# Delta rule's doubling steps: only the nonzero blocks masked, copied and multiplied

## The reference, cut to what matters

```python
kk = jnp.einsum("bhncd,bhnsd->bhncs", k, k)
a_mat = jnp.where(strict, kk * decay * beta[..., :, None], 0.0)
lhs = jnp.eye(CHUNK, dtype=jnp.float32) + a_mat
rhs = jnp.concatenate([v * beta[..., None], k * (beta * jnp.exp(G))[..., None]], axis=-1)
sol = lax.linalg.triangular_solve(lhs, rhs, left_side=True, lower=True, unit_diagonal=True)
```

## Time and profile before

| | |
|---|---|
| time, median of 3 runs | 2549.62 us (2547.74 to 2551.56) |
| profiled execution, its span (first to last instruction; no other time of it is given) | 2549.4 us |
| PE busy | 2211.0 us, 87% |
| DVE busy | 1752.8 us, 69% |
| ACT busy | 1001.0 us, 39% |
| granted TensorE clock, mean | 0.936 of 2.4 GHz |
| records of line 1352 (products of the delta rule) | 944 of 13768 on PE |

### The profile page before, as it was taken

One profiled execution on the slowest core, in us unless ns is written; L12 is line 12 of the kernel. 1 busy time (PEld: TensorE's weight loads), 2 busy tenths in 40 slices (PEclk: granted clock), 3 DMA queues, 4 the chain that ended last, 5 costly groups with the idle time before them and its releaser, 6 DMA issues.

```text
span 2549.4 us, 34445 instructions
## 1 busy us (share of the span) xinstructions
PE 2211.0 (87%) x13768; PEld 1900.7 (75%) x13768; DVE 1752.8 (69%) x3280; ACT 1001.0 (39%) x1607; POOL 806.2 (32%) x673
## 2 busy tenths in 40 slices
PE   8999999999999999999999999999998554444445
PEld 8999998999999999998999998888875221111112
DVE  6656895566556556895566556243559999899986
ACT  4446554554345446563555432443322111111111
POOL 1006871000000006871000000000037777777774
PEclk9999999999999999999999999999999777777767
DMA  7568994035555568993035554443469999999997
GB/s 244 185 173 145 188 181 137 20 119 174 183 183 172 191 163 153 178 185 133 18 118 168 191 187 155 131 143 107 162 217 407 419 419 419 418 420 419 420 419 325
DMA packets 316513, 560.29 MB, mean 220 GB/s; under 512 B 16312, under 2 KB 233410, under 8 KB 316354
## 3 DMA queue, kind: packets, MB, share of 16 engines
q1 hardware_dynamic: 242626, 289.63, 41.2%
q0 software_dynamic: 73728, 268.47, 25.9%
HBM read 557.00 MB, written 1.05 MB: 219 GB/s over the span
## 4 chain that ended last, share of the span: by engine, by line
PE 63%; DVE 17%; POOL 8%; DMA 7%; issue 3%; ACT 2%; SPq 0%; DVEq 0%; ACTq 0%; POOLq 0%
PE banks_to L945 11%; DVE banks_to L1159 7%; PE bank L459 6%; PE bank L460 6%; PE bank L461 6%; PE bank L368 6%; DMA proj<-in_peer_v,gdn_conv 4%; POOL proj L2843 4%; POOL weights L2843 3%; PE banks_and L368 3%; DMA weights<-in_peer_v,gdn_conv 3%; PE banks_to L1352 2%; PE banks_and L459 2%; PE banks_and L460 2%; PE banks_and L461 2%
## 5 line engine op out<-in xcount | busy, mean ns | idle before, releaser
L415 POOL TENSOR_TENSOR weights_low<-weights,weights_high 128x1024 fp32r<-128x1024 f32 x128 | 306.0, 2427 | 649.8 <-ACT weights_high L378 630.4
L461 PE MATMUL bank<-operand_hi,weights_low 128*128 128x256 f32 x1744 | 492.1, 282 | 0.0
L459 PE MATMUL bank<-operand_hi,weights_high 128*128 128x256 f32 x1728 | 488.7, 283 | 0.3 <-DVE gdn_conv L1244 0.2
L460 PE MATMUL bank<-operand_lo,weights_high 128*128 128x256 f32 x1728 | 487.4, 282 | 0.0
L378 ACT CAST weights_high<-weights 128x1024 fp32r<-128x1024 f32 x392 | 386.3, 1045 | 0.8 <-DMA weights<-in_ffn_w_in 0.7
L451 DVE TENSOR_TENSOR weights_low<-weights,weights_high 128x1024 fp32r<-128x1024 f32 x264 | 308.2, 1222 | 93.5 <-ACT weights_high L378 93.5
L461 PEld LDWEIGHTS bank<-operand_hi,weights_low 128*128 128x128 f32 x1744 | 330.5, 190 | 0.0
L459 PEld LDWEIGHTS bank<-operand_hi,weights_high 128*128 128x128 f32 x1728 | 327.1, 189 | 3.0 <-issue 0.8
L460 PEld LDWEIGHTS bank<-operand_lo,weights_high 128*128 128x128 f32 x1728 | 325.7, 188 | 1.2
L461 PE MATMUL banks_and<-operand_hi,weights_low 128*128 128x256 f32 x720 | 202.8, 282 | 0.0
L459 PE MATMUL banks_and<-operand_hi,weights_high 128*128 128x256 f32 x704 | 199.2, 283 | 0.3 <-DVE gdn_conv L1244 0.2
(11 more groups left out here) (574 smaller groups left out, 4675.3 us busy)
## 6 DMA issues: line engine op xcount, KB each, us to landing
weights<-in_ffn_w_in SPq DMA_DIRECT2D x88, 1024.0 KB, 5.1
weights<-in_mix_w_in SPq DMA_DIRECT2D x64, 1024.0 KB, 12.9
weights<-in_ffn_w_out SPq DMA_DIRECT2D x44, 1024.0 KB, 5.0
weights<-in_w_in SPq DMA_DIRECT2D x24, 1024.0 KB, 5.4
weights<-in_cnv_w_o SPq DMA_DIRECT2D x8, 1024.0 KB, 6.2
weights<-in_gdn_w_o SPq DMA_DIRECT2D x8, 1024.0 KB, 5.2
weights<-in_mix_w_out SPq DMA_DIRECT2D x8, 1024.0 KB, 5.0
proj<-in_peer_w_q SPq DMA_DIRECT2D x5, 1024.0 KB, 11.6
```

What stands on the lines that cost most here:

```text
L415: S.rest.by(X.gpsimd.tensor_tensor(halves(m.low[b % SLOTS])[q], halves(m.raw[b % SLOTS])[q], halves(mix_high(m, l, i))[q].bitcast(F32), AL ...
L459: t.matmul(out, w_hi, x_hi, start=start, stop=False, skip_group_check=skip)
L460: t.matmul(out, w_hi, x_lo, start=False, stop=False, skip_group_check=skip)
L461: return t.matmul(out, w_lo, x_hi, start=False, stop=stop, skip_group_check=skip)
```

## The change

Every operation of a doubling step is cut to the columns and rows that are not zero.

- The masked keys of steps 2 to 6 are packed: half the columns (64 of 128) go to the first half of `KB` (`Delta.L`). DVE masks 512 elements per partition instead of 1024.
- The first product streams only the 64 columns of T whose bit k is 0 (all steps), and from step 2 on it loads only the 64 packed columns as weights, so its result is 64 x 64. ACT copies 256 elements per group instead of 512, from step 2 on in 64 partitions.
- The transposes of steps 2 to 5 are made of the other 64 columns of T, which DVE packs with a new copy into the second half of `KB` (`Delta.Tc`); PE waits for that copy ("Tc"). The transpose has 64 partitions; ACT copies 64 partitions x 512. Step 6 transposes all of T as before.
- The second product streams 64 columns; its weights are 128 columns of `TT` as before, in steps 2 to 5 in 64 partitions. In step 6 it is 64 x 64, in partitions 64 to 127.
- DVE subtracts 256 elements per group instead of 512.

The diff, cut:

```diff
+        thin = lambda t: t.rearrange("p j n -> p (j n)").rearrange("p (half j n) -> p half j n", half=2, n=P // 2)
+        self.L, self.Tc = ([thin(B["KB"])[:, half, :, :] for B in m.delta] for half in range(2))
...
+    def bit(t, k, value):
+        return t.rearrange("p j (a two b) -> p (j a) two b", two=2, b=1 << k)[:, :, value, :]
...
+STEP = P // 2
+def step_rows(k):
+    return slice(0, P) if k == 1 else slice(STEP, P) if k == 6 else slice(0, STEP)
...
@@ vector_level
-    mask = m.level[:, k, :].unsqueeze(1).to_broadcast([P, 8, P])
-    S.delta_dve.by(X.vector.tensor_tensor(m.delta[g]["KB"], m.delta[g]["A"], mask, ALU.mult), l, "L", k, g)
+    if k < 2:
...
+    else:
+        four = lambda t: t.rearrange("p j (a b) -> p j a b", b=1 << k)
+        A = Delta.bit(m.delta[g]["A"], k, 1).rearrange("p (j a) b -> p j a b", j=8)
+        mask = Delta.bit(m.level[:, k:k + 1, :], k, 1).unsqueeze(1).to_broadcast([P, 8, STEP >> k, 1 << k])
+        ins = X.vector.tensor_tensor(four(Delta(m).L[g]), A, mask, ALU.mult)
@@ tensor_delta
-            E.by(products(X, m.four(b), lambda j: B["KB"][:, 4 * c + j, :], lambda j: B["T"][:, 4 * c + j, :]), l, "M", k, g, c)
+            out = m.four(b)[:, :, 0:STEP] if k == 1 else m.four(b)[0:STEP, :, 0:STEP]
+            keys, upper = B["KB"] if k == 1 else D.L[g], D.bit(D.ch(B["T"], c), k, 0).rearrange("p (j a) b -> p j a b", j=4)
+            E.by(products(X, out, lambda j: keys[:, 4 * c + j, :], lambda j: upper[:, j, :, :]), l, "M", k, g, c)
...
+                if k < 6:
+                    w.wait_ge(*V.at(l, "Tc", k, g, c))
...
+                        ins = t.transpose(m.four(b + 2)[0:STEP, j, :], D.Tc[g][:, 4 * c + j, :], m.ident[:, :])
...
-                E.by(products(X, m.four(b + 2), lambda j: B["TT"][:, 4 * c + j, :], lambda j: B["D"][:, 4 * c + j, :]), l, "TM", k, g, c)
+                E.by(products(X, m.four(b + 2)[:, :, 0:STEP], lambda j: B["TT"][rows, 4 * c + j, :],
+                              lambda j: B["D"][rows, 4 * c + j, 0:STEP]), l, "TM", k, g, c)
...
+                E.by(products(X, m.four(b + 2)[0:STEP, :, 0:STEP], lambda j: B["D"][rows, 4 * c + j, 0:STEP],
+                              lambda j: B["TT"][rows, 4 * c + j, STEP:P]), l, "MT", g, c)
@@ vector_delta
+                V.by(v.tensor_tensor(upper4, upper4, step, ALU.subtract), l, "T", k, g, c)
+                if k < 5:
+                    w.wait_ge(*V.at(l, "T", k, g, c))
+                    V.by(v.tensor_copy(ch(D.Tc[g], c).rearrange("p j (a b) -> p (j a) b", b=2 << k), Delta.bit(ch(B["T"], c), k + 1, 1)),
+                         l, "Tc", k + 1, g, c)
@@ scalar_delta
-            A.by(a.copy(D.ch(B["D"], c), m.four(b)), l, "M", k, g, c)
+            A.by(a.copy(D.ch(B["D"], c)[step_rows(k), :, 0:STEP], m.four(b)[out, :, 0:STEP]), l, "M", k, g, c)
...
-                A.by(a.copy(D.ch(B["TT"], c), m.four(b + 2)), l, "TT", k - 1, g, c)
+                A.by(a.copy(D.ch(B["TT"], c)[rows, :, :], m.four(b + 2)[rows, :, :]), l, "TT", k - 1, g, c)
```

More of the change, by code:

```diff
@@ L1342, in ch @@
         return t[:, 4 * c:4 * c + 4, :]
+    @staticmethod
+    def bit(t, k, value):
+        return t.rearrange("p j (a two b) -> p (j a) two b", two=2, b=1 << k)[:, :, value, :]
 GC = [(g, c) for g in range(2) for c in range(2)]
@@ L1589, in tensor_delta @@
                 X.bank_free(b + 2)
+                if k < 6:
+                    w.wait_ge(*V.at(l, "Tc", k, g, c))
                 for j in range(4):
-                    ins = t.transpose(m.four(b + 2)[:, j, :], B["T"][:, 4 * c + j, :], m.ident[:, :])
+                    if k < 6:
+                        ins = t.transpose(m.four(b + 2)[0:STEP, j, :], D.Tc[g][:, 4 * c + j, :], m.ident[:, :])
+                    else:
+                        ins = t.transpose(m.four(b + 2)[:, j, :], B["T"][:, 4 * c + j, :], m.ident[:, :])
                 E.by(ins, l, "turned", k - 1, g, c)
@@ L1598, in tensor_delta @@
             X.bank_free(b + 2)
+            rows = step_rows(k)
             if k < 6:
-                E.by(products(X, m.four(b + 2), lambda j: B["TT"][:, 4 * c + j, :], lambda j: B["D"][:, 4 * c + j, :]), l, "TM", k, g, c)
+                E.by(products(X, m.four(b + 2)[:, :, 0:STEP], lambda j: B["TT"][rows, 4 * c + j, :],
+                              lambda j: B["D"][rows, 4 * c + j, 0:STEP]), l, "TM", k, g, c)
                 X.free[b + 2] = [V.at(l, "T", k, g, c)]
             else:
-                E.by(products(X, m.four(b + 2), lambda j: B["D"][:, 4 * c + j, :], lambda j: B["TT"][:, 4 * c + j, :]), l, "MT", g, c)
+                E.by(products(X, m.four(b + 2)[0:STEP, :, 0:STEP], lambda j: B["D"][rows, 4 * c + j, 0:STEP],
+                              lambda j: B["TT"][rows, 4 * c + j, STEP:P]), l, "MT", g, c)
                 X.free[b + 2] = [V.at(l, "TT", 6, g, c)]
@@ L1661, in vector_delta @@
 def vector_delta(X, m, S, l):
-    v, w, conv, L = X.vector, X.dve, m.conv, m.layer[l]
+    v, w, conv, L, D = X.vector, X.dve, m.conv, m.layer[l], Delta(m)
     E, A, V, ch = S.delta_pe, S.delta_act, S.delta_dve, Delta.ch
@@ L1683, in vector_delta @@
                 w.wait_ge(*E.at(l, "TM", k, g, c))
-                V.by(v.tensor_tensor(ch(B["T"], c), ch(B["T"], c), m.four(b + 2), ALU.subtract), l, "T", k, g, c)
+                upper, step = Delta.bit(ch(B["T"], c), k, 0), m.four(b + 2)[:, :, 0:STEP].rearrange("p j (a b) -> p j a b", b=1 << k)
+                upper4 = upper.rearrange("p (j a) b -> p j a b", j=4)
+                V.by(v.tensor_tensor(upper4, upper4, step, ALU.subtract), l, "T", k, g, c)
[3 more added lines that the diff above has]
+                         l, "Tc", k + 1, g, c)
             else:
                 w.wait_ge(*E.at(l, "MT", g, c))
-                V.by(v.tensor_tensor(ch(B["TT"], c), ch(B["TT"], c), m.four(b + 2), ALU.subtract), l, "TT", 6, g, c)
+                corner = ch(B["TT"], c)[0:STEP, :, STEP:P]
+                V.by(v.tensor_tensor(corner, corner, m.four(b + 2)[0:STEP, :, 0:STEP], ALU.subtract), l, "TT", 6, g, c)
     vector_out_rest(X, m, S, l, 0)
@@ L1714, in scalar_delta @@
             w.wait_ge(*V.at(l, "QK", g, c))
-            A.by(a.copy(D.ch(B["D"], c), m.four(b)), l, "M", k, g, c)
+            out = slice(0, P) if k == 1 else slice(0, STEP)
+            A.by(a.copy(D.ch(B["D"], c)[step_rows(k), :, 0:STEP], m.four(b)[out, :, 0:STEP]), l, "M", k, g, c)
             if k > 1:
+                rows = step_rows(k) if k < 6 else slice(0, P)
                 w.wait_ge(*E.at(l, "turned", k - 1, g, c))
-                A.by(a.copy(D.ch(B["TT"], c), m.four(b + 2)), l, "TT", k - 1, g, c)
+                A.by(a.copy(D.ch(B["TT"], c)[rows, :, :], m.four(b + 2)[rows, :, :]), l, "TT", k - 1, g, c)
         if k < 6:
```

3 lines of the change are left out of this document (added).

## The result

| | before | changed |
|---|---|---|
| median | 2550.63 us (5 runs) | 2564.93 us (5 runs, 2555.48 to 2566.57) |
| ratio to before | | 1.0049, 95% interval 1.0039 to 1.006 |
| span of the profiled execution | 2549.4 us | 2557.2 us (its time 2558.63) |
| granted clock, mean of the profiled execution | 0.936 | 0.931 |

The forecast was 2543.0 us, faster, with 2532 to 2558 as the range. The kernel became slower. The five times of the changed kernel lie 11 us apart, those of before 4, and their mean clocks go from 0.931 (2558.63 and 2555.48 us) to 0.924 (2566.57 us): the ratio in the table is the one on record for these runs, and that of the two medians is 1.0056. By either the kernel is slower by about half a per cent, clear of the noise.

The account below looks back on a forecast made before the run. PE was taken to bound the kernel: 10.1 us gained on narrow products less 6.8 us for form changes is 3.3 us per layer, 6.6 for both, giving 2543.0 us from 2549.6; range 2532 to 2558 us.

Parts of the forecast that it names:

- What bounds the kernel: In the steps PE has no idle time; only PE's work, waits or pace move the end.
- The pace of a record: On PE, a record gets cheaper only if loaded and streamed columns both shrink: 0.059 us at 64, against 0.111.
- The gain of 0.42 per group: First products of steps 2 to 6 and step 6's second products: 24 groups, 10.1 us per layer.
- the form change of 0.13: Narrow products alternate with full-form transposes in steps 2 to 6: 10 changes per step, 6.8 us lost per layer.
- the sum: Over the steps, 10.1 less 6.8 gives 3.3 us per layer, 6.6 for both: 2543.0 us.
- DVE and ACT: Masks, subtractions and copies in the steps stay covered by PE; DVE goes from 5.2 to 4.35 us per step.
- the fourth rival: Less dense PE work in the steps lowers the granted clock; eight spells give 2556 us; chance 0.12.
- the fewer rows: Second products on 64 partitions load the same number of columns, so they stay at 0.89 us per group: gain 0.
- the eight spells of the text: Half-clock spells of 3.4 us, each losing 1.6 us in the steps; eight in all give 2556 us.
- Third rival: Each form change in the steps costs a record's whole latency, 0.275 us: slower, 2556.9 us; chance 0.15.
- First and second rival: No form changes with narrow transposes: 2535.8 us, chance 0.17; changes free or second products shrink too: 2532 us, chance 0.08.
- Fifth rival: Gains and gaps in the steps cancel: within 0.2%, the lower edge of the forecast's own case; no separate chance.

Follow-up runs that it names:

- the run with 72 columns: Changed kernel with second products streaming 128 columns; first products of steps 2 to 6 also load 72 columns instead of 64: 2535.49 us, ratio 0.9946.
- the wide kernel: Changed kernel, but second products of steps 1 to 5 stream 128 columns, and step 1's first products all of T: 2543.21 us, ratio 0.9979.
- the one with all rows: Kernel loading 72 columns with ACT's other work moved earlier, plus second products of steps 2 to 5 on 128 rows, unused ones cleared: 2533.17 us, ratio 0.9936.

## Why the prediction was wrong

**What bounds the kernel: right.** PE's pace in the steps decided every run.

**The pace of a record: right.** 0.059 was forecast and 0.058 measured; the second products stayed at 0.89 per group; neither side alone helps. The gain of 0.42 per group and the form change of 0.13 (measured 0.12 to 0.15, and 0.19 at the change of rows) gave 3.3 us per layer; with the clock held up the gain was 66.62 - 63.58 = 3.04, and the time 2543.21, where 2543.0 stood. That is a match of the sum in a kernel with wide second products, not of the forecast for this one. The reading of the earlier trace rows, that transposes run in the full form and that the narrow products change form 10 times a step, is what the run with 72 columns showed.

**DVE and ACT: right.** Covered, with the durations taken.

**The step that failed is the granted clock: the sum takes 1.00 throughout, the fourth rival, given 0.12, was the case that occurred, and the fewer rows were costed at nothing.** The price of a spell was near (1.6 us for 3.4 us at half clock); there was more of it than the eight spells of the text. The clock cost about 7.06 us in layer 0 and 10.16 in layer 1 of the profiled execution (span 2557.2), where the sum had a gain of 6.6 for both; the slower executions were up to 8 us longer, at a lower mean clock. The evidence was misread in three ways. The earlier trace rows show 40 loaded columns at full clock, but those products use 128 rows and stream 256 columns, so they say nothing of products that use half of both. The text weighed "loads and gaps", while the runs show that the size of the second products counts, rows and streamed columns together: the gaps and narrow first products of the wide kernel did no harm, and full first products did not protect. And the fewer rows stand in the words "The fewer rows (64 partitions) change nothing in the number of columns loaded". That holds for the pace, and for the clock it was most of the harm: the same edit with 128 rows is 2544.4 us, with other numbers in the unused rows. Not all of it: the spell in step 1 of layer 1 had no product on 64 rows before it in its stretch.

Three smaller readings were wrong and changed nothing. The 0.275 us for a record's latency is the mean duration of a product record of line 1352, not in the earlier trace rows. Step 5 of layer 0 began at 493.55 us, not 493.3. And the fillers of the earlier trace rows do not start at the fast pace: 24 in 3.17 us is 0.13 each, and the first stand 0.21 apart (9.40, 9.62, 9.83 us), so they do not show that transposes alone had raised the clock.

The Trainium skill's page "TensorE: Matmul & The Clock Gate", HAM oscillation, ties the fall of the clock to idle PE; here the trace disagrees, since PE has no idle time between 458.37 and 529.01 us and the clock is 0.88. Its Part 4, on transposes, was not tested: they were the same in number in every run. The Trainium skill's page "TensorEngine Tiling (Array Packing)", Key Properties, has the drain at a change of form; the trace agrees, at 0.12 to 0.19 us each, and that was priced rightly.

**Third rival** (each change costs 0.275): wrong, 0.12 to 0.19. **First and second rival** (changes free or fewer): wrong as read, though the run with 72 columns reaches the first one's time (2535.49, forecast 2535.8) and the one with all rows nearly the second's (2533.17, forecast 2532) by really removing the changes. **Fifth rival** (no change): wrong, the kernel is slower beyond its interval.

What stays open is where between these sizes the clock begins to fall, why it fell in step 1 of layer 1 on 128 rows and not in the same step elsewhere, and why one kernel with wide second products lost it in step 6 of layer 1.

## What to carry to other kernels

Cutting zeros out of small f32 products paid on TensorE only where loaded and streamed columns both shrank, and a little more than 64 loaded columns (72 here) was better than 64, since it saves a gap at every neighbour. Streamed columns and rows that ride free under a load of 128 columns should stay: they cost no time here, and cutting both of them took away the clock. When a change makes work smaller without making it shorter, look at the granted clock of its stretch before any sum of durations.

## What the runs showed that was not expected

- The granted clock fell to half with PE busy all the time: 64 rows and 64 streamed columns against 128 loaded ones, 0.50 in the window of 473.23 to 478.35 us. With either at 128 it stayed at 1.00 in steps 2 to 5. In step 1 of layer 1 it fell to 0.50 with 128 rows too (0.83 in the window of 1223.87 to 1227.80 us), in one stretch of several with that step.
- Half the partitions save ACT nothing: 585 ns for a copy of 64 x 512 elements, 586 for 128 x 512.
- A group's first product with 72 loaded columns is faster in its place (0.51 us) than one with 64 (0.61).
- Behind the same 2.08 us of idle PE the clock fell in one execution and not in the next (0.51 and 1.00), which moves a time by some 1.5 us.
